# Retention with V centred at its transposition and the cross decay divided out

## The chip, the cores and the metric

The kernel runs on one NeuronCore of a Trainium2 chip, as one launch. The metric is the device time of that launch in microseconds. The core has a matrix engine (TensorE, PE in the rows; its weight loads are PEld), a vector engine (VectorE, DVE), a scalar engine (ScalarE, ACT), GpSimd (POOL) and a queue engine (SyncE, SP) that issues the DMA transfers. They run side by side and meet at semaphores.

## What is computed

A two-layer backbone over 1024 latent tokens and 256 context tokens (1280 in all). Each layer mixes tokens in four head groups behind one input projection, then has a SwiGLU FFN. The change touches one of the four groups, bidirectional chunkwise retention: 4 heads of width 64, chunks of 128 tokens, forward and backward. Its core in the reference:

```python
def _ret_out(qc, kc, vc, s_prev):
    ...
    dmat = jnp.where(dist >= 0, jnp.exp(lg[:, None, None] * jnp.maximum(dist, 0.0)), 0.0)
    scores = jnp.einsum('bhncd,bhnmd->bhncm', qf, kf) * dmat[None, :, None]
    y = jnp.einsum('bhncm,bhnme->bhnce', scores, vf)
    cross_decay = jnp.exp(lg[:, None] * (j + 1.0))
    y = y + jnp.einsum('bhncd,nbhde->bhnce', qf, s_prev) * cross_decay[None, :, None, :, None]

def _head_layer_norm(y, dtype, eps=1e-6):
    mu = jnp.mean(y, axis=-1, keepdims=True)
    var = jnp.mean(jnp.square(y - mu), axis=-1, keepdims=True)
    yn = (y - mu) * lax.rsqrt(var + eps)
```

The state `s_prev` of a chunk is the decayed sum of K^T V over the chunks before it. The normalised outputs of both directions are multiplied by their gates and added. In layer 0 all 10 chunks (tiles) of 128 tokens get an output, in layer 1 only the 8 latent ones.

## The kernel before

All streams are written by hand: each engine has its own program, and `S[...]` are the semaphores between them. `at(name, l)` is the semaphore's count at the start of layer `l`. Activations lie with channels on the partitions and tokens along the row; the retention works with tokens on the partitions, tile by tile (`t` is the tile, `n` its place in the loop, `tq` the first tile with an output, `h` the head, `dr` the direction).

The retention has two stages in each layer. The first builds the states, tile by tile. PE transposes V and K of a tile (`tok_turn`, L810), ACT takes them out of PSUM, DVE weights V by its decay to the chunk's end (`weighted`, L1660 and L1661), PE forms K^T V (`products`, L824), and DVE and ACT add and store the states (L1674, L1174).

The second stage is the output loop, on which the prediction rests. For a tile:

- PE, `inner_scores` (L848): four products of K and Q, one per head, into banks 0 and 4. Each uses the 64 rows of one head; odd heads lie in the upper 64 rows.
- DVE, `masks` (L1700): two multiplications of the scores with the decay tables `dmask`, which give `pmask`, 128x128 for each head and direction.
- PE, `retained_out`: four products of Q with the states of both directions (L863, 64 rows, 128 columns, banks 2 and 5), and then, after the masks, eight products of `pmask` with V (L869, 128 rows, 64 columns, bank 1).
- DVE, `centre` (L1709 to L1718): the state part times the cross decay, plus the inner part, the sum over each head, the mean, and the subtraction. It raises `y_mid`.
- ACT (L1205): the square. DVE, `variance` (L1722, L1723). POOL (L1945): the power -1/2. DVE, `normalise` (L1727).
- PE, `turned_out` (L880): four transposes into bank 3. DVE, `gated` (L1734, L1735): times the gates, then the sum of the directions. ACT (L1195) and DVE (L1740) split the result in two halves of 16 bits.

The engines run these in an order written out in loops. PE: outputs of tile `t`, transposes of tile `t-1`, scores of tile `t+1`. DVE: `masks(n)`, `gated(n-2)`, `variance(n-1)`, the forward state of a later tile (L1691), `gated_lo(n-2)`, `normalise(n-1)`, `centre(n)`. When the last tile is stored, SP loads the tables of the attention (L488 to L490), and the next products of PE wait for them.

```python
                    for n in range(NQ + 2):
                        ...
                        if 1 <= n <= NQ:
                            normalise(n - 1)
                        if n < NQ:
                            centre(n)
```

## Time and profile before

| | us |
|---|---|
| median of 3 runs | 3718.29 |
| the three runs | 3718.29, 3709.38, 3722.48 |
| the profiled execution, its own time | 3710.92 |
| its span in the profile | 3709.1 |
| mean granted clock of TensorE | 0.881 of 2.4 GHz |

The profile shows one execution. Its page gives each engine's busy time and the costliest groups of instructions; the trace behind it can be asked for a timeline, for one line's instructions, and for the busy time in chosen stretches. PEclk is the clock that TensorE was granted, 1.00 for 2.4 GHz and 0.50 for 1.2 GHz. A matmul on 32-bit numbers shows as two load records and two product records, a transpose as one of each. "idle before" is the time that the engine had nothing to do before the row, with what ended it; "issue" means nothing that the profile shows. The output loop lies at about 416 to 508 us in layer 0 and 2372 to 2446 us in layer 1.

### The profile page before, as it was taken

The numbers are of one execution on the slowest core, as the hardware profiler recorded it, in microseconds if no ns is written. First come the engines' busy times: TensorE is split into PE (matmuls) and PEld (weight loads), VectorE is DVE, ScalarE is ACT, GpSimd is POOL, SyncE is SP. The second block draws the span as 40 slices with busy tenths as digits, with TensorE's granted clock in tenths as the row PEclk, the third lists the DMA queues.
The fourth block names the chain that finished last, engine by engine and source line by source line (L and its number), as shares of the span: only waits on it lengthen the run. The fifth ranks groups of instructions, "written<-read, shape, count | busy, mean of one in ns | idle before, by whom it ended". The sixth has DMA issues, their size and how long they took to land.

```text
span 3709.1 us, 45803 instructions
## 1 busy us (share of the span) xinstructions
PE 3221.3 (87%) x17774; PEld 1859.2 (50%) x17774; DVE 1846.1 (50%) x2565; ACT 1045.0 (28%) x1514; POOL 301.9 (8%) x208
## 2 busy tenths in 40 slices
PE   6798778777889999999999489679787899999997
PEld 6344544566454665555545234445666444444443
DVE  1794745788447211222225595746776364122235
ACT  2311213444344111111113311214444353111122
POOL 2400000000121000000002230000000210000001
PEclk8999669566889999999999699778666999999998
DMA  4110010011112321111111100011111222111112
GB/s 182 48 41 17 6 36 35 35 45 45 50 53 89 115 91 63 40 36 44 40 51 63 56 35 35 6 42 46 57 57 40 80 90 103 51 50 47 51 57 102
DMA packets 59451, 206.87 MB, mean 56 GB/s; under 512 B 7360, under 2 KB 8384, under 8 KB 59328
## 3 DMA queue, kind: packets, MB, share of 16 engines
q1 hardware_dynamic: 58176, 199.89, 15.1%
q10 hardware_dynamic: 1152, 5.24, 0.4%
q8 instruction: 89, 1.46, 0.2%
q14 instruction: 34, 0.28, 0.0%
HBM read 200.91 MB, written 4.19 MB: 55 GB/s over the span
## 4 chain that ended last, share of the span: by engine, by line
PE 54%; issue 26%; DVE 13%; ACT 5%; POOL 1%; DMA 0%; SPq 0%; POOLq 0%; DVEq 0%; ACTq 0%
PE PS L555 49%; DVE R L1578 4%; DVE wlo L1317 2%; PE PS L740 1%; ACT X L1031 1%; ACT R L1029 1%; DVE R L1395 1%; PE PS L613 1%; DVE R L1382 1%; ACT whi L984 1%; POOL st L1945 1%; PE PS L796 1%; DVE R L1700 1%; PE PS L586 1%; DVE X L1674 0%
## 5 line engine op out<-in xcount | busy, mean ns | idle before, releaser
L555 PE MATMUL PS<-R,whi 128*128 128x512 f16 (+1 forms) x7808 | 2131.5, 360 | 121.8 <-DVE wlo L1317 50.1
L555 PE MATMUL PS<-R,wlo 128*128 128x512 f16 (+1 forms) x3904 | 1404.7, 360 | 0.0
L555 PEld LDWEIGHTS PS<-R,whi 128*128 128x128 f16 x7808 | 765.8, 99 | 902.8 <-issue 68.7
L1317 DVE SCALAR_TENSOR_TENSOR wlo<-stage,whi 128x1024 f16<-128x1024 f32 (+1 forms) x260 | 332.0, 1277 | 513.5 <-ACT whi L984 495.7
L555 PEld LDWEIGHTS PS<-R,wlo 128*128 128x128 f16 x3904 | 385.2, 99 | 382.2 <-issue 17.8
L984 ACT ACTIVATE whi<-stage 128x1024 f16<-128x1024 f32 (+1 forms) x260 | 268.7, 1034 | 183.5 <-PE PS L555 133.6
L1876 POOL TENSOR_TENSOR X<-X 128x512 f32<-128x512 f32 (+2 forms) x105 | 154.6, 1475 | 1755.7 <-ACT X L1248 1611.2
L1578 DVE SCALAR_TENSOR_TENSOR R<-X,small,R 128x1024 f32<-128x1024 f32 (+1 forms) x180 | 219.1, 1267 | 1.8
L1816 DVE SCALAR_TENSOR_TENSOR X<-X,PS 128x512 f32<-128x512 f32 (+3 forms) x60 | 62.0, 1034 | 305.6 <-PE PS L555 305.5
L650 PE MATMUL PS<-ident,R 128*128 128x128 f32 x656 | 146.9, 374 | 74.1 <-DVE R L1440 46.9
L1811 DVE SCALAR_TENSOR_TENSOR X<-X,PS 128x512 f32<-128x512 f32 (+3 forms) x60 | 62.1, 1035 | 297.5 <-ACT X L1265 297.5
L1416 DVE TENSOR_REDUCE tiny<-PS 128x1 f32<-128x1280 f32 (+1 forms) x144 | 196.8, 1367 | 15.9 <-PE PS L632 14.2
L632 PE MATMUL PS<-R 128*128 128x512 f16 (+1 forms) x400 | 146.5, 492 | 59.6 <-DVE R L1427 53.9
L1057 ACT ACTIVATE R<-PS,tiny 128x1280 f32<-128x1280 f32 (+1 forms) x144 | 177.6, 1233 | 49.7 <-DVE tiny L1420 48.5
L1269 ACT ACTIVATE R<-X 128x512 f16<-128x512 f32 (+7 forms) x60 | 54.4, 906 | 450.1 <-DVE X L1816 450.0
L1068 ACT ACTIVATE R<-PS 128x512 f16<-128x512 f32 (+1 forms) x200 | 97.1, 518 | 268.9 <-PE PS L650 268.8
L650 PEld LDWEIGHTS PS<-ident,R 128*128 128x128 f32 x656 | 105.1, 195 | 106.5 <-DVE R L1440 47.8
L1427 DVE TENSOR_TENSOR R<-PS,R 128x512 f16<-128x512 f32 (+1 forms) x200 | 112.9, 592 | 73.8 <-ACT R L1068 73.2
L1265 ACT ACTIVATE X<-PS 128x512 f32<-128x512 f32 (+3 forms) x60 | 52.3, 872 | 304.4 <-PE PS L555 304.4
L664 PEld LDWEIGHTS PS<-X,R 128*128 128x128 f16 x1968 | 113.8, 130 | 25.0 <-issue 15.2
L664 PE MATMUL PS<-X,R 128*128 128x64 f16 x1968 | 115.1, 237 | 4.0 <-DVE R L1427 4.0
L677 PEld LDWEIGHTS PS<-csil,X 128*128 128x128 f32 x768 | 113.1, 233 | 1.0 <-issue 0.8
(183 smaller groups left out, 2517.6 us busy)
## 6 DMA issues: line engine op xcount, KB each, us to landing
stage<-in_w_gu SPq DMA_DIRECT2D x120, 512.0 KB, 3.4
X<-in_w_ada SPq DMA_DIRECT2D x60, 512.0 KB, 3.5
stage<-in_w_down SPq DMA_DIRECT2D x48, 512.0 KB, 3.5
stage<-in_w_in SPq DMA_DIRECT2D x44, 512.0 KB, 3.5
stage<-in_w_out SPq DMA_DIRECT2D x32, 512.0 KB, 3.5
T<-in_w_ada SPq DMA_DIRECT2D x20, 512.0 KB, 3.5
R<-in_w_ada SPq DMA_DIRECT2D x16, 512.0 KB, 10.4
stage<-in_w_down SPq DMA_DIRECT2D x16, 384.0 KB, 2.9
```

Source lines behind the costliest of these rows:

```text
L555: last = mm(slot(j, t0, t1)[:, c0 - t0:c1 - t0], w[:, j, k, :], row, start=(k == 0 and q == 0), stop=(k == K - 1 and q == 2))
L632: last = mm(slot(c)[:, k0:k1], Qst[:, 2 * h + c, bass.ds((t_first + r) * P, P)], Kst[:, 2 * h + c, k0:k1], start=True, stop=True)
L650: last = nc.tensor.transpose(o[:, i * P:(i + 1) * P], Wt[h % 2][:, (k0 + i) * P:(k0 + i + 1) * P], ident[:, :])
L664: last = mm(PS[:, 7, h * DV:(h + 1) * DV], WTb(h, p)[:, x, i * P:(i + 1) * P], Vst[:, k0 + i, h, v, :], start=(k0 + i == 0 and q == 0), st ...
L677: last = mm(PSF[:, bass.ds(2 * ADA_PER[l] * r + (ADA_COL + 2 * i), 2)], ring[j][:, k * P:(k + 1) * P], csil[:, k, :], start=(k == 0), stop ...
L984: A(whi[:, j, 0:K, :], stage[:, j, 0:K, :], ACT.Copy, scale=WS).then_inc(S["w_hi"], 1)
L1057: A((P1, P2)[c][h % 2][:, 0:keys], slot(c)[:, 0:keys], ACT.Exp, scale=SCORE, bias=nbias[:, h % 2, c:c + 1], accum_out=den[:, h % 2, c:c + ...
L1317: STT(wlo[:, j, 0:K, :], stage[:, j, 0:K, :], WS, whi[:, j, 0:K, :], ALU.mult, ALU.subtract).then_inc(S["w_lo"], 1)
L1416: own.link(RED(smax[:, h % 2, c:c + 1], slot(c)[:, 0:keys], AX.X, ALU.max))
L1427: TT(WTb(h, p)[:, 1, 0:w], turned(p, w), WTb(h, p)[:, 0, 0:w], ALU.subtract).then_inc(s("wt_lo"), 1)
L1578: STT(acc, src, wv, acc, ALU.mult, ALU.add).then_inc(S["conv"], 1)
L1876: TT(xrow(0)[:, a0:a1], xrow(0)[:, a0:a1], xrow(2 + d % 2)[:, a0:a1], ALU.add).then_inc(S[used], 1)
```

## The change

V is transposed by a matmul against `centre`, a matrix that also subtracts from each head's 64 values their mean; K is still transposed. Products with a centred V have mean 0 over the head, so the outputs need no mean and no subtraction. The outputs of a row are also no longer multiplied by the cross decay: the decay tables are divided by it instead, once per layer (eight operations on `dmask`), and since the norm takes out a factor of the row, only its epsilon has to be scaled (`eps_z`). The state part and the inner part can then be summed in PSUM: per head and direction one product with the state opens the sum and one with the mask closes it. The sums lie in banks 1 and 2 or 5 and 6, by turns. ACT squares them and DVE normalises them straight from PSUM. `centre(n)` on DVE is gone, as is `y_mid`.

```diff
--- before.py
+++ after.py
@@ -141,6 +141,7 @@
         bada = sb("bada", [P, 48])
         per_tok = sb("per_tok", [P, 2, NTILE])
         tiny = sb("tiny", [P, 44])
+        centre = sb("centre", [P, P])
...
-        st8 = sb("st8", [P, 4, 8])
+        spare = X[:, 3 * PADW + TOK:4 * PADW]
+        st8 = spare[:, 0:32].rearrange("p (a g) -> p a g", a=4)
+        eps_z = spare[:, 32:40]
...
-        ycross = RB[:, 2048:2560]
...
+        undecay, inv_cross = rtab[:, 0:8], T[:, 800:808]
+        Y_BANKS = (1, 5)
+
+        def y_psum(n):
+
+            b = Y_BANKS[n % 2]
+            return PS[:, b:b + 2, 0:256].rearrange("p x (g e) -> p x g e", g=4)
...
@@ -800,15 +810,20 @@
...
+                        if l == 0:
+                            pe.wait_ge(S["small_const"], 4)
...
-                    for q, row in enumerate((G + 2, G + 3, G, G + 1)):
-                        last = nc.tensor.transpose(PS[:, (6, 3)[i % 2], q * P:(q + 1) * P], R[:, row, t * P:(t + 1) * P],
-                                                   ident[:, :])
+                    for q in range(2):
+                        mm(PS[:, (6, 3)[i % 2], q * P:(q + 1) * P], R[:, G + 2 + q, t * P:(t + 1) * P], centre[:, :],
+                           start=True, stop=True)
+                    for q in range(2, 4):
+                        last = nc.tensor.transpose(PS[:, (6, 3)[i % 2], q * P:(q + 1) * P],
+                                                   R[:, G + q - 2, t * P:(t + 1) * P], ident[:, :])
                     last.then_inc(S["tr_ps"], 1)
...
@@ -851,23 +866,22 @@
 
                 def retained_out(t):
                     n = t - tq
-                    if n:
-                        pe.wait_ge(S["y_mid"], at("y_mid", l) + n)
+                    if n >= 2:
+
+                        pe.wait_ge(S["y_norm"], at("y_norm", l) + n - 1)
                     if t == 0:
                         pe.wait_ge(S["states_zero"], at("states_zero", l) + 1)
                     else:
                         pe.wait_ge(S["state_fwd"], at("state_fwd", l) + t)
+                    pe.wait_ge(S["masked"], at("masked", l) + n + 1)
                     for h in range(HB):
-
                         b, q = 64 * (h % 2), h // 2
-                        mm(PS[:, 2 + 3 * (h % 2), 0:256].rearrange("p (d c) -> p d c", d=2)[:, :, q * 64:(q + 1) * 64],
-                           R[b:b + 64, G + 4 + q, t * P:(t + 1) * P],
-                           states[b:b + 64, :, t, q * 64:(q + 1) * 64], start=True, stop=True)
-                    pe.wait_ge(S["masked"], at("masked", l) + n + 1)
-                    for dr in range(2):
-                        for h in range(HB):
-                            last = mm(PS[:, 1, dr * 256 + h * 64:dr * 256 + (h + 1) * 64], pmask[:, dr, h, :],
-                                      vtok[:, t, h * 64:(h + 1) * 64], start=True, stop=True)
+                        bank = Y_BANKS[n % 2] + h % 2
+                        for dr in range(2):
+                            y = PS[:, bank, dr * P + q * 64:dr * P + (q + 1) * 64]
+                            mm(y, R[b:b + 64, G + 4 + q, t * P:(t + 1) * P], states[b:b + 64, dr, t, q * 64:(q + 1) * 64],
+                               start=True, stop=False)
+                            last = mm(y, pmask[:, dr, h, :], vtok[:, t, h * 64:(h + 1) * 64], start=False, stop=True)
                     last.then_inc(S["y_ps"], 1)
 
...
@@ -1198,11 +1212,11 @@
                 for n in range(NTILE - tq):
                     if n >= 2:
                         gated_hi(n - 2)
-                    act.wait_ge(S["y_mid"], at("y_mid", l) + n + 1)
+                    act.wait_ge(S["y_ps"], at("y_ps", l) + n + 1)
                     if n:
 
                         act.wait_ge(S["y_var"], at("y_var", l) + n)
-                    A(SW[:, 0:512], ysum[n % 2], ACT.Square).then_inc(S["y_sq"], 1)
+                    A(SW[:, 0:512].rearrange("p (x g e) -> p x g e", x=2, g=4), y_psum(n), ACT.Square).then_inc(S["y_sq"], 1)
...
@@ -1545,6 +1559,15 @@
             lo_part(0, 0, UK[0])
             dve.wait_ge(S["consts"], 32)
             inverse_root(0)
+            own.link(nc.vector.reciprocal(inv_cross, cross))
+            TS(undecay, inv_cross, DK ** -0.5, None, ALU.mult)
+            STT(eps_z.rearrange("p (x g) -> p x g", x=2), inv_cross.rearrange("p (g x) -> p x g", x=2), 1e-6,
+                inv_cross.rearrange("p (g x) -> p x g", x=2), ALU.mult, ALU.mult)
+            own.link(nc.vector.tensor_copy(centre[:, :], ident[:, :]))
+            dve.wait_ge(S["small_const"], 3)
+            for b in (0, 64):
+                last = TS(centre[b:b + 64, b:b + 64], ident[b:b + 64, b:b + 64], -1.0 / 64, None, ALU.add)
+            last.then_inc(S["small_const"], 1)
...
@@ -1678,10 +1701,8 @@
 
                 tq = t0 // P
                 NQ = NTILE - tq
-                y8 = lambda n: ysum[n % 2].rearrange("p (g e) -> p g e", g=8)
+                y8 = lambda n: ysum[n % 2].rearrange("p (g x e) -> p x g e", g=4, x=2)
                 s8 = SW[:, 0:512].rearrange("p (g e) -> p g e", g=8)
-                c8 = ycross.rearrange("p (g e) -> p g e", g=8)
-                b8 = lambda ap: ap.rearrange("p (g e) -> p g e", e=1).to_broadcast([P, 8, 64])
...
@@ -1702,29 +1723,18 @@
                                   dmask[:, :, x:HB:2, :], ALU.mult)
                     last.then_inc(S["masked"], 1)
 
-                def centre(n):
-
-                    dve.wait_ge(S["y_ps"], at("y_ps", l) + n + 1)
-                    for x in range(2):
-                        last = TT(c8[:, x:8:2, :], PS[:, 2 + 3 * x, 0:256].rearrange("p (g e) -> p g e", g=4),
-                                  cross[:, x:8:2].rearrange("p (g e) -> p g e", e=1).to_broadcast([P, 4, 64]), ALU.mult)
-                    own.link(last)
-                    if n >= 2:
-
-                        dve.wait_ge(S["yt_ps"], at("yt_ps", l) + n - 1)
-                    own.link(TT(ysum[n % 2], PS[:, 1, :], ycross, ALU.add))
-                    own.link(RED(st8[:, 0, :], y8(n), AX.X, ALU.add))
-                    own.link(TS(st8[:, 1, :], st8[:, 0, :], 1.0 / 64, None, ALU.mult))
-                    TT(y8(n), y8(n), b8(st8[:, 1, :]), ALU.subtract).then_inc(S["y_mid"], 1)
-
                 def variance(n):
                     dve.wait_ge(S["y_sq"], at("y_sq", l) + n + 1)
                     own.link(RED(st8[:, 2, :], s8, AX.X, ALU.add))
-                    TS(st8[:, 3, :], st8[:, 2, :], 1.0 / 64, 1e-6, ALU.mult, ALU.add).then_inc(S["y_var"], 1)
+                    STT(st8[:, 3, :], st8[:, 2, :], 1.0 / 64, eps_z, ALU.mult, ALU.add).then_inc(S["y_var"], 1)
 
                 def normalise(n):
                     dve.wait_ge(S["y_pow"], at("y_pow", l) + n + 1)
-                    TT(y8(n), y8(n), b8(st8[:, 2, :]), ALU.mult).then_inc(S["y_norm"], 1)
+                    if n >= 2:
+
+                        dve.wait_ge(S["yt_ps"], at("yt_ps", l) + n - 1)
+                    TT(y8(n), y_psum(n), st8[:, 2, :].rearrange("p (x g e) -> p x g e", x=2, e=1).to_broadcast([P, 2, 4, 64]),
+                       ALU.mult).then_inc(S["y_norm"], 1)
 
...
@@ -1746,6 +1756,12 @@
                 for t in range(1, tq + 1):
                     forward_state(t)
                 dve.wait_ge(S["d_tab"], at("d_tab", l) + 16)
+                for d in range(2):
+                    for h in range(HB):
+
+                        last = TS(dmask[:, d, h, :], dmask[:, d, h, :], 0.0, undecay[:, 4 * d + h:4 * d + h + 1],
+                                  ALU.is_gt, ALU.mult)
+                own.link(last)
...
@@ -1759,8 +1775,6 @@
                         gated_lo(n - 2)
                     if 1 <= n <= NQ:
                         normalise(n - 1)
-                    if n < NQ:
-                        centre(n)
```

On PE, the products of one steady tile of the output loop stand like this before (L848 scores, L863 with the states, L869 with the masks, L880 transposes; `y_mid` is raised by `centre` on DVE, `masked` by the masks):

```order
L848 MATMUL PS<-R 128x128 [waits masked]
L848 MATMUL PS<-R 128x128 x3
L863 MATMUL PS<-X,R 128x2x64 [waits state_fwd,y_mid]
L863 MATMUL PS<-X,R 128x2x64 x3
L869 MATMUL PS<-X,R 128x64 [waits masked]
L869 MATMUL PS<-X,R 128x64 x7
L880 MATMUL PS<-ident,T 128x128 [waits yb_sum,y_norm]
L880 MATMUL PS<-ident,T 128x128 x3
```

And now (L863 scores, L882 with the states, L884 with the masks, L894 transposes):

```order
L863 MATMUL PS<-R 128x128 [waits masked]
L863 MATMUL PS<-R 128x128 x3
L882 MATMUL PS<-X,R 128x64 [waits masked,state_fwd,y_norm]
L884 MATMUL PS<-X,R 128x64
L882 MATMUL PS<-X,R 128x64
L884 MATMUL PS<-X,R 128x64
...
L894 MATMUL PS<-ident,T 128x128 [waits yb_sum,y_norm]
L894 MATMUL PS<-ident,T 128x128 x3
```

Eight pairs of L882 and L884 stand there, two of them shown. The four state products that stood ahead of the wait for the masks are eight now, behind it, and one by one between the eight of the masks.

On DVE, from one `normalise` (L1727) to the next masks (L1700) and the gating behind them, before:

```order
L1727 TENSOR_TENSOR T<-T,st 128x512 [waits y_pow]
L1709 TENSOR_TENSOR R<-PS,tiny 128x4x64 [waits y_ps]
L1709 TENSOR_TENSOR R<-PS,tiny 128x4x64
L1715 TENSOR_TENSOR T<-PS,R 128x512 [waits yt_ps,dve_own]
L1716 TENSOR_REDUCE st<-T 128x8 [waits dve_own]
L1717 TENSOR_SCALAR st<-st 128x8 [waits dve_own]
L1718 TENSOR_TENSOR T<-T,st 128x512 [waits dve_own]
L1700 TENSOR_TENSOR R<-PS,R 128x4x128 [waits y_ps,sc_ps]
```

And now (L1736 is `normalise`, L1721 the masks, L1744 the gating, L1728 and L1729 the variance, L1712 the forward state):

```order
L1736 TENSOR_TENSOR T<-PS,X 128x2x4x64 [waits yt_ps,y_pow]
L1721 TENSOR_TENSOR R<-PS,R 128x4x128 [waits y_ps,sc_ps]
L1721 TENSOR_TENSOR R<-PS,R 128x4x128
L1744 TENSOR_TENSOR R<-PS,R 128x4x128 [waits yt_ps]
L1745 TENSOR_TENSOR R<-R 128x2x128 [waits dve_own]
L1728 TENSOR_REDUCE X<-SW 128x8 [waits y_sq]
L1729 SCALAR_TENSOR_TENSOR X<-X 128x8 [waits dve_own]
```

The six operations between the normalisation and the masks are gone; the masks follow at once, with their wait for the scores.

## Rows read from the trace of the kernel before

**Rows 1.** The page, part 1: busy time, share of the span, instructions.
```profile
PE 3221.3 (87%) x17774; PEld 1859.2 (50%) x17774; DVE 1846.1 (50%) x2565; ACT 1045.0 (28%) x1514; POOL 301.9 (8%) x208
```

**Rows 2.** Table by stretches, layer 0: busy us by engine (records), PEclk, DMA share, GB/s.
```profile
397.00:416.00 19.00, 13.94 (x106) 11.94 (x106) 17.20 (x55) 10.54 (x36) 0.00 (x0) 1.00 0.09 29
416.00:422.00 6.00, 3.78 (x40) 3.33 (x40) 3.40 (x8) 0.00 (x0) 0.00 (x0) 1.00 0.00 0
422.00:430.00 8.00, 6.60 (x36) 6.00 (x36) 5.93 (x14) 0.63 (x1) 1.65 (x1) 0.55 0.00 0
430.00:498.00 68.00, 56.26 (x284) 47.59 (x280) 57.64 (x126) 8.37 (x16) 13.19 (x8) 0.50 0.00 1
```

**Rows 3.** Timeline of one tile of the output loop: start, length, engine, line, idle before.
```profile
437.00 1.12 PE L880 MATMUL PS<-ident,T 128*128 128x128 f32 x4 [0.63 <-DVE T L1727]
...
438.05 0.93 PEld L848 LDWEIGHTS PS<-R 64*128 64x128 f32 x8 [0.33 <-issue]
438.05 1.23 PE L848 MATMUL PS<-R 64*128 64x128 f32 x8
...
439.91 1.28 DVE L1700 TENSOR_TENSOR R<-PS,R 128x512 f32<-128x512 f32 x2
...
440.05 1.22 PE L863 MATMUL PS<-X,R 64*128 64x128 f32 x8 [0.77 <-DVE T L1718]
441.11 0.68 DVE L1734 TENSOR_TENSOR R<-PS,R 128x512 f32<-128x512 f32 x1
...
441.25 3.67 PE L869 MATMUL PS<-X,R 128*128 128x64 f32 x16
...
442.17 0.68 DVE L1722 TENSOR_REDUCE st<-SW 128x8 f32<-128x512 f32 x1
...
442.96 0.48 DVE L1691 SCALAR_TENSOR_TENSOR X<-X,tiny 128x64 f32<-128x64 f32 x2
...
444.80 0.69 DVE L1727 TENSOR_TENSOR T<-T,st 128x512 f32<-128x512 f32 x1 [1.03 <-POOL st L1945]
...
448.45 1.28 DVE L1700 TENSOR_TENSOR R<-PS,R 128x512 f32<-128x512 f32 x2
```

**Rows 4.** The masked product L869 by its line: ns min/median/max.
```profile
L869 PE MATMUL PS<-X,R x288: 275/421/476, 418.2 to 2434.4; 128*128 128x64 f32 x144
```

**Rows 5.** Timeline of the first tile of the loop in layer 0.
```profile
415.98 0.71 PE L848 MATMUL PS<-R 64*128 64x128 f32 x8 [0.74 <-ACT X L1174]
...
416.83 1.29 DVE L1700 TENSOR_TENSOR R<-PS,R 128x512 f32<-128x512 f32 x2 [1.16 <-PE PS L848]
...
418.17 2.00 PE L869 MATMUL PS<-X,R 128*128 128x64 f32 x16 [1.03 <-DVE R L1700]
...
420.10 0.72 PE L848 MATMUL PS<-R 64*128 64x128 f32 x8
...
423.40 1.23 PE L863 MATMUL PS<-X,R 64*128 64x128 f32 x8 [2.58 <-DVE T L1718]
```

**Rows 6.** Timeline of the end of the loop in layer 0.
```profile
493.63 2.55 PE L869 MATMUL PS<-X,R 128*128 128x64 f32 x11
...
500.89 0.68 DVE L1722 TENSOR_REDUCE st<-SW 128x8 f32<-128x512 f32 x1
...
507.61 1.69 SPq L488 DMA_DIRECT2D X<-in_ropeA  x2
```

**Rows 7.** Timeline of one turn of the stage that builds the states.
```profile
408.55 0.71 PE L824 MATMUL PS<-T 128*128 128x128 f32 x4 [0.40 <-DVE SW L1661]
...
409.73 0.42 DVE L1660 TENSOR_TENSOR T<-X,tiny 128x256 f32<-128x256 f32 x1
```

**Rows 8.** Timeline of DVE in the first 110 us.
```profile
11.67 0.29 DVE L1527 TENSOR_TENSOR T<-T 128x128 f32<-128x128 f32 x1 [11.67 <-DMA ones<-in_ones]
...
82.35 0.19 DVE L1507 TENSOR_TENSOR T<-PS,bada 128x32 f32<-128x32 f32 x1 [25.28 <-PE PS L740]
```

**Rows 9.** Timeline of DVE ahead of the loop in layer 1.
```profile
2371.55 1.00 DVE L1691 SCALAR_TENSOR_TENSOR X<-X,tiny 128x64 f32<-128x64 f32 x4 [0.19 <-ACT X L1174]
```

More of the change, by code:

```diff
@@ L236, in build @@
             state_fwd=NTILE - 1,
-            sc_ps=NTILE, masked=NTILE, y_ps=NTILE, y_mid=NTILE, y_sq=NTILE, y_var=NTILE, y_pow=NTILE, y_norm=NTILE,
+            sc_ps=NTILE, masked=NTILE, y_ps=NTILE, y_sq=NTILE, y_var=NTILE, y_pow=NTILE, y_norm=NTILE,
             yt_ps=NTILE, yb_sum=NTILE, yb_hi=NTILE, yb_done=NTILE,
```

## Prediction

> **What bounds the kernel now.** The page gives PE 87% of the span and DVE 50% [rows 1]. Such averages say nothing of the stage that is changed, so I read, in this order: the table by stretches, the timeline of one tile of the retention's output loop, the same loop's first tile, its end, and the stage ahead of it. The loop runs 10 tiles in layer 0 and 8 in layer 1, and layer 1's rows have the same lengths.
>
> In the table [rows 2] PE is granted 1.00 of its 2.4 GHz while the states are built and in the loop's first tile, 0.55 in the next stretch and 0.50 (1.2 GHz) for the rest of the loop, though PE shows 56.26 of 68 us busy there and DVE 57.64. Two engines look alike full, so the timeline must tell which one sets the pace. One tile takes 8.54 us: the masks (L1700) start at 439.91 and the next ones at 448.45 [rows 3]. DVE goes from the masks' end (441.19) through gating (441.11) and variance (442.17) to the normalisation, 444.80 to 445.49, and then through the operations of `centre` to the next masks, with one wait of 1.03 us, for POOL's power. So the loop is DVE's chain, and PE waits for it, 0.77 us before L863. PE's products after the masks (L869, 3.67 us) end at 444.92, ahead of the normalisation.
>
> **Part 1: what DVE loses.** `centre` goes: from 445.49 to the masks at 448.45 that is 2.96 us a tile, on the path today. What is late next? In the new order PE does its 16 small products only after the masks, then the four transposes of the tile before, then the next scores, and only these release the next masks. DVE's remaining chain after the masks is 445.49 - 441.19 = 4.3 us. If PE's products last longer than that, DVE's gain is worth nothing in the loop, and the new tile is PE's sum.
>
> **Part 2: what PE gets.** Before, a tile has 4 state products of 64 rows by 128 columns (L863) and 8 of 128 rows by 64 columns (L869). Each matmul has two load and product records, since L869 shows 288 of each for 18 tiles x 8 [rows 4]. At the low clock the 16 of one tile take 3.67 us; the first lasts 0.476, the longest of its kind, so the 15 further steps are (3.67 - 0.476)/15 = 0.213 us each. L863's 8 records take 1.22 us, since neighbours there lie in different halves of the rows and go in pairs. Now there are 8 state products, each followed by a masked product that uses all rows: 32 records, none with a neighbour in the other half. I take the full step for each: 32 x 0.213 = 6.8 us. The two ends: 0.107 for the 16 with 64 rows, as in pairs (5.1 us in all), and 0.213. I take the upper one, since a record without a partner in the other half has nothing to share the step with. A page on the same matter: the Trainium skill, "TensorE: Matmul & The Clock Gate", section "LDWEIGHTS (loading the stationary operand)", has the load's time depend on columns and not on rows; by it the sum is the one I take, by the pair price it would be 31 us lower over 18 tiles. No run so far shows a lone one.
>
> **Part 3: going from 128 rows to 64 and back.** PE does so about twice a tile now and 15 times within the 16 products afterwards. The price can be seen once a tile: after the last transpose the loads for the scores (L848) start late, "0.33 <-issue", with their semaphore long given [rows 3]. The transposes end at 437.00 + 1.12 = 438.12, four paired steps later it would be 438.97, and the scores end at 439.28: 0.30 us for the switch. At the full clock L869 ends at 420.17 and the scores at 420.82 against 420.17 + 4 x 0.107 = 420.60: 0.22 us [rows 5]. Part of the 0.30 is particular to that place: both loads of the first pair come one behind the other (0.107), and the products ahead have 128 columns where the new ones have 64 (some 0.05). So I take 0.14 a switch, and keep 0 (the other direction shows no such row) and 0.30 as ends. Per tile 15 x 0.14 = 2.1 us. The Trainium skill says the same against this change ("TensorEngine Tiling (Array Packing)", "Key Properties"): changing the tiling mode, not just the tile, drains TensorE. It gives no time. By it the forecast stands; without it the switches are free, which is the second rival below.
>
> **The new tile**, from the masks' end at 1.2 GHz: 0.05 to the first product, 6.8 + 2.1 for the 32 records, 0.85 for four transposes, 0.30 for the switch, 0.85 for the scores, 0.21 for the last one's end, 0.14 until DVE starts (416.69 to 416.83 in [rows 5]), 1.28 for the masks: 12.6 us, 4.06 more than 8.54. DVE's 4.3 us and ACT's square lie beside PE's 8.9.
>
> **Part 4: both ends of the loop.** Ahead of it DVE now rewrites the decay tables in 8 operations of 128x128. Nearest rows: 0.29 for a first product of 128x128 alone [rows 8], and 0.48 for L1691's two operations of 0.28, so 0.2 apart [rows 3]. I take 1.8 us (1.5 to 2.3). In layer 0 DVE had waited 1.16 us for the scores before its first masks at 416.83 [rows 5]: free from 415.67, it would be done at 417.6, so 0.8 us show. In layer 1 updates of the forward state fill that gap [rows 9], nothing hides the new operations, and I take 1.9 us with the wait for the last. The first masks were followed by L869 alone, ending 3.34 us after the masks' start (420.17 - 416.83), since L863 had run beforehand; now 1.29 + 0.05 + 8.9 + 0.2 = 10.4, so 7.1 more, at the low clock. PE then stands idle over 2 us before it, and in the old order the clock fell to 1.2 GHz around a wait of 2.58 us [rows 2, 5]. Were the first tile still at 2.4 GHz, 3 us a layer less. The first interval has no transposes to do: -0.4. The tail: before, from PE's end (496.18) to the table load that waits for the last tile (507.61) 11.4 us [rows 6]. Now transposes 1.2, gating 1.07 (441.11 to 442.17), then from the variance on the old 6.7 (500.89 to 507.61): 9.0, so -2.4.
> Layer 0: 0.8 + 7.1 + 9 x 4.06 - 0.4 - 2.4 = 41.6. Layer 1: 1.9 + 7.1 + 7 x 4.06 - 0.4 - 2.4 = 34.6. Sum +76 us.
>
> **Costed at nothing.** V's two transposes per tile become matmuls with `centre`: two more records each tile, 0.21 us; PE waits 0.40 us before L824 there and DVE's operations have no idle time between them [rows 7], so DVE's pace covers it; without that cover it is 20 x 0.21 = 4 us. The six new operations at the start lie in the 25.28 us ahead of 82.35 in which DVE waits for the modulation products [rows 8]. ACT's square reads PSUM, beside PE's work. SP and POOL get nothing new; POOL's power waits as before.
>
> The profiled execution took 3710.9 us (span 3709.1), the three runs have a median of 3718.3, 7 higher. Median + 76 gives **3794**.
>
> **Rivals.**
> 1. PE stays at 2.4 GHz and switches are free: then 32 records take 3.6 us, DVE's 4.3 is the longer one and the tile is 1.28 + 4.3 + 0.06 + 0.43 + 0.22 + 0.43 + 0.16 + 0.14 = 7.0 us. 16 x -1.5, first tiles +3.6, tables +2.7, tails -6: -24, **3694**, faster. It decides where the granted clock does not fall in the loop. For it: 1.00 in the stretches with 73% PE busy ahead. Against: the fall in the old order at the second tile, and no rise at 83% busy [rows 2]. 7%. With dear switches at 2.4 GHz the tile is about 8.5 and the sum +4: 5%.
> 2. Low clock, free switches: 15 x 0.14 x 18 = 38 less: +38, **3756**. For it: the direction 64 to 128 is seen nowhere. 15%.
> 3. Low clock, every switch at the seen 0.30: 15 x 0.16 x 18 = 43 more: +119, **3837**. For it: that is the only row. 18%.
> 4. Low clock, free switches and lone 64-row records at the pair price: 38 - 31 = +7, **3725**: 5%.
> The forecast has 50%.
>
> **Range and chances.** About 0.3% (11 us) is what a measurement here can tell from no change. 3745 to 3840 takes in the forecast, rivals 2 and 3 and leaves some 17 in 100 below. Faster: 0.07. Same: rival 4 and the full clock with dear switches, less what of them falls outside, 0.08. Slower: 0.85.
>
> **What would show it.** Masks 12.6 us apart; the 16 products a block of 9 us with PEld idle by "issue" between loads; DVE waiting for the scores before each mask, some 5 us a tile; PEclk 0.50 through the loop; the state stage unchanged. Wrong if the clock stays at 1.00, if the block takes under 7 us, or if DVE's normalisation still ends after PE's block.

## The result, and the profile after

| | before | after |
|---|---|---|
| median, us (4 runs each) | 3715.44 (3709.38 to 3722.48) | 3799.72 (3793.99 to 3806.4) |
| ratio after / before, 95% interval | | 1.0235 (1.0217 to 1.0252) |
| profiled execution, us (its span) | 3710.9 (3709.1) | 3795.99 (3794.2) |

The change costs 84 us; the prediction was +76 (3794), with a range of 3745 to 3840. The page, part 1, of the kernel after, beside [rows 1]: PE has 93 us more of busy time and 184 more instructions, DVE 46 us less.

```profile
PE 3314.2 (87%) x17958; PEld 1927.6 (51%) x17958; DVE 1799.7 (47%) x2479; ACT 1044.0 (28%) x1514; POOL 301.7 (8%) x208
```

Lines of the kernel after that are not named yet: L1762 the decay tables, L1219 ACT's square, L1188 ACT's copy of the states. The same stretches as in [rows 2]; columns as there:

```profile
397.00:416.00 19.00, 15.03 (x120) 12.99 (x118) 17.83 (x61) 10.10 (x34) 0.00 (x0) 1.00 0.09 29
416.00:422.00 6.00, 4.59 (x16) 3.80 (x16) 1.65 (x4) 0.00 (x0) 0.00 (x0) 0.59 0.00 0
422.00:430.00 8.00, 6.52 (x27) 5.19 (x26) 1.48 (x3) 0.60 (x1) 0.00 (x0) 0.50 0.00 0
430.00:498.00 68.00, 60.58 (x224) 48.66 (x224) 22.09 (x50) 4.75 (x10) 8.19 (x5) 0.50 0.00 1
```

In the fourth row DVE has fallen from 57.64 to 22.09 us of 68, while PE does 224 records where it did 284 and shows more busy time for them. That is what a slow record rate looks like: the records follow each other later, and inside the block of products the engine shows no idle time for it. The clock is at its lower level, 1.2 GHz, from within the first tile, one stretch earlier than before. In narrower stretches it is 1.00 from 416 to 417 us and 0.54 from 417 to 418, so it fell while PE waited for the first masks.

Timeline of one tile after (start, length, engine, line, idle before), which answers to [rows 3]:

```profile
441.92 1.29 DVE L1721 TENSOR_TENSOR R<-PS,R 128x512 f32<-128x512 f32 x2 [8.86 <-PE PS L863]
...
443.36 0.66 PE L882 MATMUL PS<-X,R 64*128 64x64 f32 x2 [1.48 <-DVE R L1721]
...
444.56 0.69 PE L882 MATMUL PS<-X,R 64*128 64x64 f32 x2
...
445.18 0.69 PE L884 MATMUL PS<-X,R 128*128 128x64 f32 x2
...
445.79 0.69 PE L882 MATMUL PS<-X,R 64*128 64x64 f32 x2
...
446.81 0.69 DVE L1736 TENSOR_TENSOR T<-PS,X 128x512 f32<-128x512 f32 x1 [1.02 <-POOL X L1959]
...
452.57 0.69 PE L884 MATMUL PS<-X,R 128*128 128x64 f32 x2
...
453.05 1.06 PE L894 MATMUL PS<-ident,T 128*128 128x128 f32 x4
...
454.05 1.23 PE L863 MATMUL PS<-R 64*128 64x128 f32 x8
455.32 1.29 DVE L1721 TENSOR_TENSOR R<-PS,R 128x512 f32<-128x512 f32 x2 [7.82 <-PE PS L863]
```

A tile is 455.32 - 441.92 = 13.40 us. DVE is done with its part at 447.5 (446.81 + 0.69) and then waits 7.82 us for PE's scores. From a state product to the masked one and on to the next state product are 0.62 and 0.61 us, by turns, through all sixteen products: 9.69 us from the first of them to the transposes. Two full steps are 0.43, so each change of kind costs 0.19, the same in both directions. (A masked product adds to the sum that the state product just before it wrote. That is not what costs: the way back, to a state product that opens another sum, takes as long.)

The new operations on the decay tables, the end of the loop in layer 0, and the first wait, of [rows 5] and [rows 6], after:

```profile
414.28 1.66 DVE L1762 TENSOR_SCALAR R<-R,tiny 128x128 f32<-128x128 f32 x8 [0.24 <-ACT X L1188]
...
415.97 1.29 DVE L1721 TENSOR_TENSOR R<-PS,R 128x512 f32<-128x512 f32 x2
...
417.41 0.66 PE L882 MATMUL PS<-X,R 64*128 64x64 f32 x2 [2.35 <-DVE R L1721]
...
546.38 0.69 PE L884 MATMUL PS<-X,R 128*128 128x64 f32 x2
...
555.75 0.81 SPq L498 DMA_DIRECT2D X<-in_ropeA  x2
```

**Where the time went.** From the last state update to the load of the rotary table (the loop with its two ends) layer 0 took 92.2 us before and 142.0 after, layer 1 75.2 and 116.1: together 90.7 us more. The rest of the span is 5.5 us shorter in this execution (1.6 ahead of the first loop, 2.4 between the loops, 1.5 behind the second), in places where nothing that bounds was edited; the cause is open.

### The profile page after: what moved, and what is told of

Read it like the earlier page. It is cut to its first block, busy times and chain, and to the rows that moved or that the text cites. A ratio compares the mean times of both kernels' runs of the same rounds, so it can differ in the third digit from the quotient of the medians.

```text
span 3794.2 us, 46089 instructions
## 1 busy us (share of the span) xinstructions
PE 3314.2 (87%) x17958; PEld 1927.6 (51%) x17958; DVE 1799.7 (47%) x2479; ACT 1044.0 (28%) x1514; POOL 301.7 (8%) x208
## 4 chain that ended last, share of the span: by engine, by line
PE 58%; issue 25%; DVE 11%; ACT 5%; POOL 1%; DMA 0%; SPq 0%; POOLq 0%; DVEq 0%; ACTq 0%
PE PS L565 48%; DVE R L1601 3%; PE PS L882 2%; PE PS L884 2%; DVE wlo L1331 2%; PE PS L750 1%; ACT X L1045 1%; ACT R L1043 1%; DVE R L1409 1%; PE PS L623 1%; DVE R L1396 1%; ACT whi L998 1%; DVE R L1721 1%; PE PS L596 1%; PE PS L863 0%
## 5 line engine op out<-in xcount | busy, mean ns | idle before, releaser
L882 PE MATMUL PS<-X,R 64*128 64x64 f32 x288 | 98.3, 443 | 29.3 <-DVE R L1721 29.3
## 6 DMA issues: line engine op xcount, KB each, us to landing
R<-in_w_ada SPq DMA_DIRECT2D x16, 512.0 KB, 10.4
```

The lines of the kernel that those rows point to most:

```text
L882: mm(y, R[b:b + 64, G + 4 + q, t * P:(t + 1) * P], states[b:b + 64, dr, t, q * 64:(q + 1) * 64], start=True, stop=False)
```

## Experiments

Each is an edit of the kernel after unless said otherwise, and those keep V centred and the cross decay divided out. The line numbers shift with the edits; the text names the operations. "Tile" is the distance of two masks in the steady part of layer 0's loop, "loops" the sum of both layers' stretches as above (167.4 us before, 258.1 after). Differences are medians against the runs of the kernel before that were made on the same chip.

### 1 and 2. The eight state products first, then the eight masked ones

Inside the block one change between 64 and 128 rows is left of fifteen. In the first the state products go through one half of the rows and then the other, in the second the halves alternate. As a sum in PSUM is now open while others begin in its bank, only the first product of each bank carries `start=True`. The diff is that of the first; the second has `for dr in range(2) for h in range(HB)` in its list instead.

```diff
-                    for h in range(HB):
...
+                    for h, dr in [(h, dr) for h in (0, 2, 1, 3) for dr in range(2)]:
...
+                        mm(y, R[b:b + 64, G + 4 + q, t * P:(t + 1) * P], states[b:b + 64, dr, t, q * 64:(q + 1) * 64],
+                           start=(q == 0 and dr == 0), stop=False)
+                    for dr in range(2):
+                        for h in range(HB):
...
+                            last = mm(y, pmask[:, dr, h, :], vtok[:, t, h * 64:(h + 1) * 64], start=False, stop=(dr == 1 and q == 1))
```

Expected of the first:

> The changed kernel, but after the wait for the masks all eight state products come first, sorted so that neighbours lie in the same half of the rows, and then the eight masked ones. Same 32 records, one way from 64 to 128 rows instead of 15 changes. Theory S (each change costs 0.19 us at 1.2 GHz, a lone record its full step of 0.213): a tile goes from 13.4 to 10.7 us, in all 18 x 2.66 = 48 us less, 3752. Rival A (what costs is that a product adds to a sum in PSUM, or eight state products instead of four): no change, 3800. Rival P (unpaired records cost nothing extra, all is change-over): the same time as the run with alternating halves.

Expected of the second:

> As the sorted run, but the eight state products alternate between the lower and the upper half of the rows. Theory S: the changes go and the 16 records run in pairs, 16 x 0.107 = 1.7 us less a tile again: tile 9.0 us, 3721. Rival A: 3800. Rival P: equal to the sorted run.

Measured: the first 3743.93 us, ratio to before 1.0082 (1.0060 to 1.0103), tile 9.95, loops 195.8. The second 3721.11, ratio 1.0031 (1.0019 to 1.0043), tile 9.07, loops 180.0. The state products (L880) and the masked products (L886) in the timeline of the first, and then of the second:

```profile
456.53 2.85 PE L880 MATMUL PS<-X,R 64*128 64x64 f32 x16 [1.48 <-DVE R L1723]
...
459.31 3.67 PE L886 MATMUL PS<-X,R 128*128 128x64 f32 x16
```

```profile
454.77 1.97 PE L880 MATMUL PS<-X,R 64*128 64x64 f32 x16 [1.48 <-DVE R L1723]
...
456.67 3.67 PE L886 MATMUL PS<-X,R 128*128 128x64 f32 x16
```

In the second the masked products start 1.90 us after the state products: 16 paired steps of 0.107 are 1.71, and the one change costs 0.19, as in the kernel after. So the order that alternates row modes is a cause by itself at this clock: the same 32 records, regrouped, give back 4.3 of 13.4 us per tile and 78 of the 91 us in the loops. With 14 changes of 0.19 fewer (2.7 us), the pairs' half steps are the other 1.7. The one change that is left leads to a masked product that adds to a sum written several products before, and it costs the same 0.19.

The first was faster than its expected tile of 10.7, because its upper half's records do not wait for the lower half's. The table by stretches for these products alone (busy us, records) shows it:

```profile
456.50:457.35 0.85, 0.82 (x4) 0.85 (x5) 0.50 0.00 0
457.35:458.20 0.85, 0.85 (x10) 0.85 (x9) 0.50 0.07 19
```

Within one half a record starts every 0.21 us (4 in 0.85, the first stretch). In the second stretch the records of both halves count. A record counts in each stretch that it touches, so 2 of the 10 had begun in the first, and 8 begin there, two every 0.21 us. So a record of 64 rows without a partner does cost the full step, as Part 2 of the prediction took it. The Trainium skill ("TensorE: Matmul & The Clock Gate", "LDWEIGHTS (loading the stationary operand)") has a load's time depend on columns and not on rows; these rows agree, with 0.21 us for a record of 64 rows as for one of 128.

### 3 and 4. Four grouped state products, ahead of the wait; scores ahead of the transposes

Both directions of a head fit into one state product of 128 columns, as in the kernel before. In 3 these four products stand ahead of the wait for the masks. In 4 also the next tile's scores and state products are issued ahead of the last tile's transposes. The diff is that of 4, shortened; the wait for the masks stands behind `from_states` in both.

```diff
+                def from_states(t):
...
+                    for h in range(HB):
...
+                        mm(PS[:, Y_BANKS[n % 2] + h % 2, 0:256].rearrange("p (d c) -> p d c", d=2)[:, :, q * 64:(q + 1) * 64],
+                           R[b:b + 64, G + 4 + q, t * P:(t + 1) * P],
+                           states[b:b + 64, :, t, q * 64:(q + 1) * 64], start=(q == 0), stop=False)
...
                     retained_out(t)
-                    if t > tq:
-                        turned_out(t - tq - 1)
                     if t < NTILE - 1:
                         inner_scores(t + 1)
+                        from_states(t + 1)
+                    if t > tq:
+                        turned_out(t - tq - 1)
```

Expected of 3:

> The changed kernel with the four state products of the old order (both directions at once) ahead of the wait for the masks, and only the eight masked products behind it, adding to the same sums. Theory S: PE's block behind the masks is back at 3.7 us and DVE's chain of 4.3 us sets the pace, then transposes, scores and masks: 8.0 us a tile, about 3701, slightly faster than the kernel before. Rival A: the block stays long, over 3760.

Expected of 4:

> As the group of four, and PE does the next scores and the next state products before the transposes of the tile before, so that the next masks wait for neither the normalisation nor the transposes. Theory S: per tile PE has 3.4 + 0.3 + 0.85 + 0.85 + 0.2 + 0.85 = 6.5 us at 1.2 GHz, DVE 1.3 + 4.3 = 5.6; 6.5 us a tile, about 3677. If DVE's chain still runs through the transposes: 8 us a tile, as the group of four. If the clock rises, DVE's 5.7: about 3663.

Measured: 3 took 3697.15 us, ratio 0.9958 (0.9943 to 0.9973), tile 7.96, loops 156.9. 4 took 3689.04, ratio 0.9936 (0.9917 to 0.9955), tile 6.75, loops 142.1. Both beat the kernel before, by 0.4% and 0.6%. In the timeline of 3 (L1738 normalise, L896 transposes, L1723 masks) the pace is again DVE's, in series with PE's transposes and scores:

```profile
461.32 0.69 DVE L1738 TENSOR_TENSOR T<-PS,X 128x512 f32<-128x512 f32 x1 [1.02 <-POOL X L1961]
...
462.06 1.12 PE L896 MATMUL PS<-ident,T 128*128 128x128 f32 x4 [0.61 <-DVE T L1738]
...
463.11 1.23 PE L863 MATMUL PS<-R 64*128 64x128 f32 x8
...
464.39 1.29 DVE L1723 TENSOR_TENSOR R<-PS,R 128x512 f32<-128x512 f32 x2 [2.38 <-PE PS L863]
```

Normalising releases the transposes, the scores queue behind them, and the masks wait 2.38 us for the scores. In 4 that wait is gone. Its tile is still 0.25 longer than expected, as the timeline shows (L877 state products, L1727 masks, L898 transposes, L1750 gating):

```profile
457.09 0.93 PEld L877 LDWEIGHTS PS<-X,R 64*128 64x128 f32 x8 [0.31 <-DVE T L1742]
457.09 1.23 PE L877 MATMUL PS<-X,R 64*128 64x128 f32 x8
457.12 1.29 DVE L1727 TENSOR_TENSOR R<-PS,R 128x512 f32<-128x512 f32 x2
...
458.25 1.12 PE L898 MATMUL PS<-ident,T 128*128 128x128 f32 x4
...
459.40 0.69 DVE L1750 TENSOR_TENSOR R<-PS,R 128x512 f32<-128x512 f32 x1 [0.99 <-PE PS L898]
```

A tile's state products write the banks that the normalising of the tile two before it reads (L1742), so they start only behind it, 0.31 us after their loads could have, and the transposes behind them: DVE waits 0.99 us for the transposes before it gates. I had left that queue out of the estimate.

### 5. Four more reductions per tile on DVE, in the kernel after

```diff
                         normalise(n - 1)
+                        for _ in range(4):
+                            own.link(RED(st8[:, 0, :], RB[:, 0:512].rearrange("p (g e) -> p g e", g=8), AX.X, ALU.add))
```

Expected:

> The changed kernel with four more reductions of the decay table by VectorE in every tile, after the normalising and beside TensorE's products: 4 x 0.7 = 2.9 us more of VectorE per tile, about what the removed centring took. Theory (after the change TensorE's order of products sets the pace, and VectorE stands idle for 7.8 us of every 13.4-us tile): no change against the changed kernel, about 3800 us. Rival (VectorE's chain is still a part of the path): 18 x 2.9 = 52 us more, about 3852 us.

Measured: 3805.89 us, 89 above before, ratio 1.0240 (1.0213 to 1.0266), which covers the 1.0235 of the kernel after. The tile is 13.45 where it was 13.40, and each loop is 2 us longer, most of it at its end, where nothing covers the last tile's reductions. Timeline:

```profile
451.63 2.83 DVE L1779 TENSOR_REDUCE X<-R 128x8 f32<-128x512 f32 x4
...
459.58 1.29 DVE L1721 TENSOR_TENSOR R<-PS,R 128x512 f32<-128x512 f32 x2 [5.12 <-PE PS L863]
```

The 2.83 us come out of DVE's wait (7.82 before them, 5.12 with them). DVE's work is worth next to nothing in the kernel after: as much as the centring had can be added for 4 us in both loops together, so its removal earned no more there.

### 6. Filler products in the kernel after, to keep TensorE at 2.4 GHz

```diff
+                def filler(k):
+                    for _ in range(k):
+                        mm(PS[:, 7, 0:P], ones[:, :], ones[:, :], start=True, stop=True)
...
                             last = mm(y, pmask[:, dr, h, :], vtok[:, t, h * 64:(h + 1) * 64], start=False, stop=True)
+                            if dr == 0 or h < HB - 1:
+                                filler(1)
...
                 inner_scores(tq)
+                filler(16)
...
                         inner_scores(t + 1)
+                        filler(4)
```

Expected:

> The changed kernel with filler products of ones by ones into a bank that nobody reads (16 ahead of the first tile, 4 behind each tile's scores, one between each two pairs of the sixteen short products). If the granted clock stays at 1.00 through the tiles, the same records run at half the time: tile about 10.2 us instead of 13.4, 18 x 3.2 = 58 us less, about 3742 us; this says that the low clock is a good part of the loss. If the clock falls all the same (0.50), the fillers only add their records: 11 x 0.21 = 2.4 us or more per tile, 3840 us or above.

Measured: 3838.42 us, ratio 1.0325 (1.0296 to 1.0355), loops 298.5. The granted clock did not hold. Table by stretches:

```profile
416.00:422.00 6.00, 6.00 (x49) 5.45 (x46) 2.63 (x9) 0.00 (x0) 0.00 (x0) 1.00 0.00 0
422.00:430.00 8.00, 8.00 (x40) 6.57 (x42) 0.00 (x0) 0.48 (x1) 0.00 (x0) 0.70 0.01 2
430.00:498.00 68.00, 67.61 (x304) 55.03 (x302) 21.10 (x47) 4.17 (x9) 8.19 (x5) 0.63 0.00 1
```

It fell in the second row, in the middle of the first tile's products, with PE shown busy for all of the 8 us. So the whole is inconclusive for what the low clock costs in this order. It gives the prices, though, since in layer 0 one tile (448.24 to 458.60, 10.36 us) ran at the full clock but for its first 0.8 us, and five of the others (17.62) at half. Timeline of state products (L886) and masked ones (L888), half clock and full clock:

```profile
434.28 0.69 PE L886 MATMUL PS<-X,R 64*128 64x64 f32 x2
...
434.89 0.69 PE L888 MATMUL PS<-X,R 128*128 128x64 f32 x2
...
436.04 0.69 PE L886 MATMUL PS<-X,R 64*128 64x64 f32 x2
...
450.65 0.43 PE L886 MATMUL PS<-X,R 64*128 64x64 f32 x2
...
451.01 0.43 PE L888 MATMUL PS<-X,R 128*128 128x64 f32 x2
...
451.65 0.43 PE L886 MATMUL PS<-X,R 64*128 64x64 f32 x2
```

From 64 rows to 128: 0.61 - 0.43 = 0.18 us at half clock, 0.36 - 0.21 = 0.15 at full clock. On the way from 128 to 64 a filler of 128 columns stands between, and four records take 1.15 us where their steps are 0.85, and 0.64 where they are 0.43: 0.30 and 0.21 more. Not all of that is the change. The two records of one filler, each in a timeline narrow enough to show it alone:

```profile
435.37 0.53 PE L869 MATMUL PS<-ones 128*128 128x128 f32 x1
...
435.69 0.42 PE L869 MATMUL PS<-ones 128*128 128x128 f32 x1
```

They start 0.32 apart, 0.11 more than a step, ahead of the change. From the second to the next state product (436.04) are 0.35 us, 0.14 more than a step. The kernel after has the same 0.35 behind a masked product, which has 64 columns, and behind the last transpose, which has 128 (the scores start at 454.05):

```profile
451.61 0.42 PE L884 MATMUL PS<-X,R 128*128 128x64 f32 x1
451.96 0.69 PE L882 MATMUL PS<-X,R 64*128 64x64 f32 x2
...
453.69 0.42 PE L894 MATMUL PS<-ident,T 128*128 128x128 f32 x1
```

The other 0.05 of the 0.19 lie behind the first record of the product after the change, whose second starts 0.27 us later (452.23 behind 451.96). So a change costs 0.19 whatever the columns ahead of it, and the 0.30 that [rows 3] shows ahead of the scores is that and 0.11 inside the scores.

One thing follows that no run shows by itself. In the full-clock tile the first product starts 1.43 us after the masks, a product with its change takes 0.36 (seen from 64 rows to 128 and taken for both ways), the last one is 0.27 ahead of the transposes, and from there to the next masks are 1.30. Without the fillers such a tile would be 1.43 + 15 x 0.36 + 0.27 + 1.30 = 8.4 us, an estimate, where the kernel before has 8.54. By it the new order costs its 4.9 us a tile only together with the low clock. The kernel before had the low clock as well, and there it cost nothing (experiment 9).

### 7. Filler products in version 4

```diff
                 from_states(tq)
+                filler(16)
...
                         inner_scores(t + 1)
+                        filler(5)
                         from_states(t + 1)
```

Expected:

> The version with four grouped state products and the next tile's scores ahead of the transposes (3689 us, tile 6.75 us at a granted clock of 0.53), with 5 filler products behind the scores and 16 ahead of the first tile. If they hold the granted clock at 1.00: VectorE's own chain of some 5.8 us sets the tile, 18 x 0.95 = 17 us less, about 3675 us. If the clock falls to 0.50 all the same: 5 x 0.43 = 2.1 us more per tile, about 3725 us.

Measured: 3666.63 us, ratio 0.9868 (0.9843 to 0.9894), the fastest of all; tile 5.78, loops 126.4. The clock holds through the loop. Table by stretches, to 480 us:

```profile
430.00:480.00 50.00, 41.48 (x372) 36.32 (x370) 37.36 (x82) 8.62 (x18) 13.19 (x8) 1.00 0.01 1
```

The timeline (L1748 normalise, L1733 masks, L1756 gating) shows nothing left but DVE's chain, POOL's power and 0.20 us for the transposes:

```profile
454.10 0.69 DVE L1748 TENSOR_TENSOR T<-PS,X 128x512 f32<-128x512 f32 x1 [1.02 <-POOL X L1971]
454.70 1.28 DVE L1733 TENSOR_TENSOR R<-PS,R 128x512 f32<-128x512 f32 x2
...
456.18 0.69 DVE L1756 TENSOR_TENSOR R<-PS,R 128x512 f32<-128x512 f32 x1 [0.20 <-PE PS L898]
```

### 8 to 10. Which part of that gain is whose

8 is the kernel before with the scores ahead of the transposes; 9 the kernel before, its order kept, with fillers (16 ahead of the loop, 8 behind the products with V, 8 behind the scores); 10 is version 7 with the four reductions of experiment 5, placed as there. The diffs of 8, and then of 9:

```diff
                     retained_out(t)
-                    if t > tq:
-                        turned_out(t - tq - 1)
                     if t < NTILE - 1:
                         inner_scores(t + 1)
+                    if t > tq:
+                        turned_out(t - tq - 1)
```

```diff
                 inner_scores(tq)
+                filler(16)
                 for t in range(tq, NTILE):
                     retained_out(t)
+                    filler(8)
                     if t > tq:
                         turned_out(t - tq - 1)
                     if t < NTILE - 1:
                         inner_scores(t + 1)
+                        filler(8)
```

Expected of 8:

> The kernel before with one edit of the order alone: the next tile's scores are issued ahead of the last tile's transposes. Theory (before the change VectorE's chain of 8.54 us, with the centring in it, sets the tile, and TensorE's order hides behind it): no change, about 3711 us. Rival (the order of scores and transposes is worth as much here as in the version without centring, 1.2 us per tile): 18 x 1.2 = 22 us less, about 3690 us, and the removal of the centring would then have no share in that gain.

Expected of 9:

> The kernel before, with its order kept, and filler products alone: 16 ahead of the first tile, and in every tile 8 behind the products with V and 8 behind the scores. If VectorE's chain of 8.54 us sets its tile at either clock, nothing changes when they hold the granted clock at 1.00: within 0.3% of 3717 us, and the 50 us of the fastest version are then not the clock's alone. If the low clock costs the kernel before as much as the version with the new order (22 us): about 3695 us. If the clock falls in spite of them, 32 records of 0.213 us come into every tile: about 3750 us or above.

Expected of 10:

> The fastest version so far (3667 us: four grouped state products and the next scores ahead of the transposes, with filler products; tile 5.78 us) with the same four extra reductions by VectorE per tile that cost the changed kernel nothing. Theory (here VectorE's chain sets the tile, so that this is where the removed centring is earned): 18 x 2.9 = 52 us more, about 3719 us, the level of the kernel before. Rival (TensorE's order or its rate still sets the tile): the reductions lie beside it and add under 10 us.

Measured: 8 took 3713.03 us, ratio 0.9991 (0.9977 to 1.0005); 9 took 3715.56, ratio 1.0009 (0.9998 to 1.0021); 10 took 3712.86, ratio 0.9998 (0.9988 to 1.0009). In 9 the clock is at 1.00 through the loop, as the table's row has it, and the tile is 8.54 us as ever; the loops are 171.8 us, 4 longer, since the fillers delay the first tile (9.30 us where it was 6.43):

```profile
430.00:498.00 68.00, 63.03 (x558) 57.11 (x558) 58.07 (x126) 8.38 (x16) 12.74 (x9) 1.00 0.00 1
```

So neither the scores ahead of the transposes nor the full clock, each alone, is worth anything while the centring is in DVE's chain; the two together were not run. In 10 the reductions put as much into DVE's chain as the centring had (2.84 against 2.96 us), and all of the gain is gone: 168.0 us in the loops against 167.4 before. Against the kernel before they cost 48 us there (-50.0 to -1.7), and 5 (84.3 to 89.2), which the intervals do not tell from nothing, in experiment 5. Removing the centring is worth what was hoped for, but only once PE's order lets it through, and all of it only with the full clock (-21.6 without it).

| kernel | tile, us | loops, us | median less that of before |
|---|---|---|---|
| before | 8.54 | 167.4 | |
| after | 13.40 | 258.1 | +84.3 |
| 1 sorted halves | 9.95 | 195.8 | +33.3 |
| 2 halves by turns | 9.07 | 180.0 | +10.5 |
| 3 four grouped, ahead of the wait | 7.96 | 156.9 | -13.5 |
| 4 scores ahead of transposes | 6.75 | 142.1 | -21.6 |
| 5 after, with the reductions | 13.45 | 262.1 | +89.2 |
| 6 after, with fillers | 17.62 at half clock | 298.5 | +121.8 |
| 7 version 4 with fillers | 5.78 | 126.4 | -50.0 |
| 8 before, scores ahead of transposes | 8.53 | 167.3 | -3.6 |
| 9 before, with fillers | 8.54 | 171.8 | +1.0 |
| 10 version 7 with the reductions | 8.4 | 168.0 | -1.7 |

Of the 50 us of version 7 the loops hold 41. The other 9 lie in stages that no edit touches and in the spread of the runs; their cause is open.

## Why the prediction was right, and where its terms were off

- **Part 1, what DVE loses.** Right. PE's products last far longer than DVE's remaining 4.3 us, and the 2.96 us are worth next to nothing (experiment 5). DVE's wait for the scores is 7.8 us a tile; "some 5 us" in the list of signs was too little, since 12.6 less DVE's own part of about 5.6 is 7.
- **Part 2, lone records of 64 rows at the full step.** Right: 0.213 us within one half (experiment 1), 0.107 in pairs (experiment 2). Rival 4, with the pair price, falls.
- **Part 3, the change of row mode.** The mis-sized term. I took 0.14 us, measured are 0.19 in both directions (experiments 2 and 6). I had taken 0.16 off the 0.30 of [rows 3]: 0.107 for the scores' first pair, which was right, and some 0.05 for the columns of the products ahead, which was wrong, since 64 and 128 columns cost alike (experiment 6). Rivals 1 (in its form with free switches) and 2 fall, as does rival 3's 0.30 for every change. The Trainium skill ("TensorEngine Tiling (Array Packing)", "Key Properties") says that changing the tiling mode drains TensorE. The runs agree in that each change costs time, 0.19 us; what TensorE does in that time they do not show.
- **The new tile.** 12.6 predicted, 13.40 measured: 9.69 for the block where the sum had 8.9, and 3.71 for all the rest where it had 3.7. Nearly the whole error is 15 x 0.05 = 0.75 us.
- **Part 4, the ends.** Tables 1.66 us for 1.8; they push the first masks by 0.8 in layer 0 as predicted (3.10 us after the start of the last group of state updates, 2.33 before) and by 1.6 for 1.9 in layer 1. First masks to the end of their products 11.35 us for 10.4, again the changes. Tail 8.7 for 9.0.
- **The sum.** With these, layer 0: 0.8 + 8.0 + 9 x 4.86 - 0.4 - 2.7 = 49.4, measured 49.8. Layer 1: 1.6 + 8.0 + 7 x 4.86 - 0.4 - 2.7 = 40.5, measured 40.9. So the loops' forecast was 14 us too low. The total was off by only 6, because the rest of the program, assumed unchanged, was 5.5 us shorter, and because the median of the kernel before, with a fourth run, was 3 us lower than the one that I added to. That part was luck.
- **Costed at nothing.** The states' stage turns every 1.99 us as before, with V transposed by matmuls. ACT's square and the six operations at the start do not show.
- **The clock.** It fell, as the sum had it, one tile earlier than before: 0.59 in the stretch of the first tile, during PE's wait of 2.35 us for the masks. Rival 1 falls with it here, in both forms. Its form with dear changes had a tile of about 8.5 us, and experiment 6 bears that out by estimate (8.4). Experiments 7 and 9 show that its condition, the full clock, can be had in other orders; in the new order as it stands, filler products did not hold it.
- **A sign that did not show.** PEld was to stand idle by "issue" between the loads of the block. The profile puts idle time by "issue" ahead of L882 only 18 times, once a tile at the wait for the masks, and none ahead of L884; the changes show as later starts alone.

## What to carry to other kernels

When work is taken from the engine that sets the pace, sum up what the next engine does in series between its two waits before counting the gain: here the same removal earned next to nothing behind PE's new order and 48 us behind a better one at the full clock. Read the granted clock with it: a low clock that costs nothing while another engine sets the pace costs as soon as TensorE does. Count a matmul order by its record steps and by its changes between 64 and 128 rows: sort the short products by row mode, let neighbours lie in different halves of the rows, and issue what needs no mask ahead of the wait for it. If sums of several products share a PSUM bank, that sorting needs one `start` per bank rather than one per sum. (The Trainium skill states the reason, "PSUM — Partial Sum Buffer", "The four PSUM rules": a second start in a bank clears the marks of a sum still open there. No run here tried it otherwise.)

## What was not expected of the hardware

- A change between 64-row and 128-row products costs 0.19 us at 1.2 GHz, in both directions and behind products of 64 as of 128 columns, and still 0.15 at 2.4 GHz: it shrinks far less than the record step does (0.213 to some 0.11).
- Records of the upper half of the rows start while records of the lower half that come earlier in the program are still to start, as the starts of the records tell: 8 begin in the 0.85 us of the second stretch of experiment 1, against 4 in the first, within one half. The Trainium skill ("TensorE: Matmul & The Clock Gate", "Step-by-step: what each phase is for") has matmuls stay in program order; for products in different halves of the rows the trace differs, and the trace decides.
- A stretch in which PE is shown busy throughout is no assurance that the granted clock stays up: in experiment 6 it fell in a stretch with 8.00 of 8 us busy, behind one with 6.00 of 6, while in experiment 9 it stayed at 1.00 with 63.03 of 68. What the chip goes by was not tried.
